# Splitting token rows before their norm is known, and moving half of each gather behind four weight blocks

## What is computed

```python
h = rms_norm(x, norm_ffn_g)                   # x * rsqrt(mean(x*x) + EPS) * g
logits = h @ w_router + b_router              # 32 experts
top_v, top_e = top_k(logits, 4); gates = softmax(top_v)
# for each expert e, the rows of h that chose it:
hh = xb @ w1[e] + b1[e]; glu, lin = split(hh)     # w1[e]: 1024 x 2048
act = min(glu, 7) * sigmoid(1.702 * glu) * (clip(lin, -7, 7) + 1)
y = act @ w2[e] + b2[e]                       # w2[e]: 1024 x 1024
x += sum over the 4 experts of gate * y
```

## Time and profile before

| | |
|---|---|
| time, median of 3 runs | 1242.89 us (1242.62 to 1244.21) |
| profiled execution, time | 1242.38 us |
| profiled execution, span | 1240.7 us |
| PE busy | 1160.5 us, 94% of the span |
| DVE, ACT, POOL busy | 387.7, 232.3, 62.9 us |
| transfers | 466.52 MB, mean 376 GB/s over the span |

### The profile page before, as it was taken

The page is one execution under the profiler, slowest core; times in us unless marked ns, Lnnn a source line. Parts: engine busy times, 40 slices in busy tenths (PEclk is TensorE's granted clock), DMA queues, the critical chain, the costliest instruction groups (busy, mean ns, idle before and its releaser), DMA issues.

```text
span 1240.7 us, 16218 instructions
## 1 busy us (share of the span) xinstructions
PE 1160.5 (94%) x6549; PEld 577.8 (47%) x6549; DVE 387.7 (31%) x729; ACT 232.3 (19%) x405; POOL 62.9 (5%) x102
## 2 busy tenths in 40 slices
PE   7999999997999999999998989898989898989996
PEld 5778899887434344343333333332323232323332
DVE  3555768377221222212121213131121212121214
ACT  3342244144101111010111011110101110111012
POOL 5302001123000000000000000000000000000000
PEclk9999999997999999999999999999999999999999
DMA  9833399996899999999999999999999999999994
GB/s 312 258 129 102 113 327 340 360 346 263 327 428 428 427 428 429 428 428 429 428 428 429 429 427 428 429 428 428 429 428 428 429 429 428 428 429 428 428 428 169
DMA packets 79748, 466.52 MB, mean 376 GB/s; under 512 B 4384, under 2 KB 51008, under 8 KB 54912
## 3 DMA queue, kind: packets, MB, share of 16 engines
q1 hardware_dynamic: 72816, 455.36, 89.7%
q0 software_dynamic: 1504, 6.13, 1.5%
q10 hardware_dynamic: 5392, 4.54, 1.2%
HBM read 460.32 MB, written 5.70 MB: 376 GB/s over the span
## 4 chain that ended last, share of the span: by engine, by line
PE 65%; DMA 30%; DVE 2%; ACT 1%; issue 1%; SPq 0%; ACTq 0%; DVEq 0%
DMA ring<-w 30%; PE bank L1739 21%; PE bank L1774 12%; PE bank L1356 9%; PE bank L1526 5%; PE bank L1714 5%; PE bank L1694 4%; PE bank L1514 2%; PE bank L1758 1%; ACT rest L801 1%; PE bank L1695 1%; PE bank L1586 1%; DMA ring<-w_in 1%; PE bank L1611 1%; PE bank L1557 1%; PE bank L1570 1%
## 5 line engine op out<-in xcount | busy, mean ns | idle before, releaser
L1739 PE MATMUL bank<-ring,rest 128*64 128x512 f32 x2048 | 457.8, 595 | 38.1 <-DMA ring<-w 31.7
L1739 PEld LDWEIGHTS bank<-ring,rest 128*64 128x64 f32 x2048 | 142.7, 136 | 333.0 <-issue 256.0
L1774 PE MATMUL bank<-ring,rest 128*64 128x512 f32 x1024 | 226.8, 595 | 17.0 <-ACT rest L801 17.0
L1281 DVE TENSOR_SCALAR rest<-bank 128x512 f32<-128x512 f32 x32 | 22.1, 692 | 486.9 <-PE bank L1739 486.9
L1774 PEld LDWEIGHTS bank<-ring,rest 128*64 128x64 f32 x1024 | 71.3, 137 | 151.2 <-issue 134.9
L1260 DVE TENSOR_TENSOR rest<-rest,bank 128x512 f32<-128x512 f32 (+1 forms) x102 | 66.9, 680 | 227.8 <-PE bank L1714 227.7
L1356 PE MATMUL bank<-rest,ring 128*128 128x288 f32 (+1 forms) x512 | 125.4, 405 | 8.5 <-DMA ring<-w_in 8.5
L797 ACT ACTIVATE rest<-rest 128x512 f32<-128x512 f32 x32 | 20.2, 630 | 523.4 <-DVE rest L1281 523.4
L1356 PEld LDWEIGHTS bank<-rest,ring 128*128 128x128 f32 x512 | 97.6, 192 | 33.9 <-DMA ring<-w_in 8.5
L1714 PE MATMUL bank<-rest 128*128 128x512 f32 (+1 forms) x204 | 98.4, 611 | 1.3 <-ACT rest L809 1.3
L809 ACT COPY rest<-bank 64x512 f32<-64x512 f32 x64 | 37.1, 580 | 225.2 <-PE bank L1774 224.5
(11 more groups left out here) (292 smaller groups left out, 712.8 us busy)
## 6 DMA issues: line engine op xcount, KB each, us to landing
ring<-w SPq DMA_DIRECT2D x192, 2048.0 KB, 33.5
ring<-w_in SPq DMA_DIRECT2D x12, 1024.0 KB, 12.0
ring<-k_t SPq DMA_DIRECT2D x8, 1024.0 KB, 12.3
ring<-v_c SPq DMA_DIRECT2D x8, 1024.0 KB, 7.2
ring<-w_xk SPq DMA_DIRECT2D x4, 1024.0 KB, 4.9
ring<-w_xv SPq DMA_DIRECT2D x4, 1024.0 KB, 4.9
ring<-w_out SPq DMA_DIRECT2D x4, 1024.0 KB, 7.6
ring<-w_xq SPq DMA_DIRECT2D x4, 1024.0 KB, 12.6
```

The source lines that it names most:

```text
L1739: last = t.matmul(out, slots[:, k, :], w[:, col], start=False, stop=(k == KT - 1))
L1774: last = t.matmul(ps[2][CAP * ds:CAP * ds + CAP, :], actT[:, at:at + CAP], w[:, b, 512 * ds:512 * ds + 512], start=(a == 0 and b == 0), st ...
```

## The change

The rows are split as they are, without the norm's factor. The factor of each token is itself split into three bf16 parts by POOL, spread over rows (`r_rows`), and brought to the slots by a further block of matmuls with the same `sel`: it lands in bank 5, ACT copies it to `r_slot`, and DVE multiplies by gain and factor while it evacuates the gather, both banks now. The first half of the columns is split while the output projection still runs; for this the copies of the bias's split go from DVE to ACT. The sums of squares are finished by DVE and PE needs one matmul for each group of tokens. The gather is two calls: `gather(0)`, with the factor's block in it, where the whole gather stood, and `gather(1)` behind the fourth unit of w1 of the pair's first expert, ahead of `combine`.

```diff
+        hx = [m(at, 3 * HALF).bitcast(BF16).rearrange("p (s t d) -> p s t d", s=3, t=2) for at in (8448, 0)]
+        hx_c = [m(at + 3 * HALF, HALF // 2).bitcast(BF16) for at in (8448, 0)]
+        hx_hi = [[hx[half][:, 0, 0, :], hx[half][:, 0, 1, :], hx_c[half]] for half in range(2)]
...
+        r_slot = m(3328, P)
+        r_part = m(3456, 5).bitcast(BF16)[:, 0:3 * TT].rearrange("p (s t) -> p s t", s=3)
+        r_rest = m(3464, TT)
+        r_rows = m(6752, 384).bitcast(BF16).rearrange("p (s t m) -> p s t m", s=3, t=2)
+        r_rows_c = m(7136, 64).bitcast(BF16)
...
+            pool.wait_ge(yrs_done, 1)
+            link(pool.tensor_copy(r_part[:, 0, :], yrs))
+            link(pool.tensor_tensor(r_rest, yrs, r_part[:, 0, :], ALU.subtract))
+            link(pool.tensor_copy(r_part[:, 1, :], r_rest))
+            link(pool.tensor_tensor(r_part[:, 2, :], r_rest, r_part[:, 1, :], ALU.subtract))
+            link(pool.tensor_copy(r_rows, r_part[:, :, 0:2].unsqueeze(3).to_broadcast([P, 3, 2, P])))
+            for part in range(COPIES):
+                q = slice(TS * part, TS * part + TS)
+                pool.tensor_copy(r_rows_c[q], r_part[q, part, 2:3].to_broadcast([TS, P])).then_inc(r_rows_done, 1)
+                pool.wait_ge(r_rows_done, part + 1)
...
+            a.copy(b1s[0:96], b1f[0:96]).then_inc(b1_split, 1)
+            def part_of_bias(sub, rows_b, done):
+                act_e.wait_ge(b1_sub, sub)
+                a.copy(b1s[rows_b], b1f[rows_b]).then_inc(done, 1)
+            def upper_rows(n):
+                half, tt = n // TT, n % TT
+                R = ROWS_C[tt]
+                if half == 0:
+                    act_e.wait_ge(y_ev, n + 1)
+                    src = y[0:R, tt, 0:HALF]
+                else:
+                    act_e.wait_ge(y_ps, n + 1)
+                    src = ps[Y_BANK[n]][0:R, :]
+                a.copy(hx_hi[half][tt][0:R, :], src).then_inc(h_hi, 1)
+            def middle_rows(n):
...
+                elif k == 4:
+                    act_e.wait_ge(b1_split, 4)
+                    upper_rows(0)
+                    upper_rows(1)
+                elif k == 5:
+                    middle_rows(0)
+                    middle_rows(1)
+                    upper_rows(2)
+                elif k == 6:
+                    middle_rows(2)
...
+            a.activation(yrs, ps[L_BANK[0]][:, NE:NE + TT], ACT.Sqrt, bias=eps, scale=1.0 / D).then_inc(std_done, 1)
+            for n in range(TT, 2 * TT):
+                upper_rows(n)
+            act_e.wait_ge(logits_in, 2)
+            a.activation(gate, gate, ACT.Exp).then_inc(logits_exp, 1)
+            def slot_scales(nth):
+                act_e.wait_ge(rs_ps, nth)
+                a.copy(r_slot, ps[5][:, 0:P]).then_inc(rs_done, 1)
...
-                act_e.wait_ge(xg_ps, 2 * nth - 1)
-                for k in range(KT // 2):
-                    last = a.activation(xg[parity][:, k, :], ps[4][:, k * P:(k + 1) * P], ACT.Copy, scale=gain_k[:, k:k + 1])
-                last.then_inc(xg_done_a, 1)
...
+                a.copy(y[0:R, tt, HALF:D], ps[Y_BANK[TT + tt]][0:R, :]).then_inc(y_ev, 1)
+                if tt == 0:
+                    slot_scales(1)
+            for n in range(TT, 2 * TT):
+                middle_rows(n)
...
+                elif c == 4:
                     x_rows(range(2))
-                if c == 6:
+                elif c == 5:
+                    rest_part(0)
+                    rest_part(1)
                     x_rows(range(2, TT))
-            dve.wait_ge(y_std, TT)
+                    third_part(0)
+                    third_part(1)
+                    dve.wait_ge(b1_split, 4)
+                    v.memset(selGT, 0.0).then_inc(selgt_zero, 1)
+                elif c == 6:
+                    rest_part(2)
+                    third_part(2)
+            dve.wait_ge(rsq_done, KT)
+            dve.wait_ge(rsq_sum, KT - 2)
+            copies = sq_c.rearrange("p (a t) -> p a t", t=TS)
+            first, last_sq = (sq_r[:, k, SEQ:T].unsqueeze(1).to_broadcast([P, P // TS, TS]) for k in (0, KT - 1))
+            v.tensor_tensor(copies, first, last_sq, ALU.add).then_inc(rsq_sum, 1)
+            v.tensor_tensor(sq_r[:, 0, 0:SEQ], sq_r[:, 0, 0:SEQ], sq_r[:, KT - 1, 0:SEQ], ALU.add).then_inc(rsq_sum, 1)
...
+            def evac_gather(nth, parity, half):
+                dve.wait_ge(xg_ps, 2 * nth - 1 + half)
+                if half == 0:
+                    dve.wait_ge(rs_done, nth)
+                for k in range(4 * half, 4 * half + 4):
+                    last = v.scalar_tensor_tensor(xg[parity][:, k, :], ps[4 + half][:, (k % 4) * P:(k % 4 + 1) * P],
+                                                  gain_k[:, k:k + 1], r_slot, ALU.mult, ALU.mult)
+                last.then_inc(xg_done_hi if half else xg_done_lo, 1)
...
+            for n in range(TT, 2 * TT):
+                rest_part(n)
+            dve.wait_ge(wr_in, 48)
+            evac_gather(1, 0, 0)
+            for n in range(TT, 2 * TT):
+                third_part(n)
+            link(v.tensor_scalar(place[:, :, NE:NE + 2], place[:, :, 0:2], -float(CAP), None, ALU.add))
...
-                        dve.wait_ge(xg_ps, g * BODY + j + 2)
+                        evac_gather(pair + 1, (j // 2) % 2, 1)
...
-                        evac_gather(g * (BODY // 2) + j // 2 + 2, (j // 2 + 1) % 2)
+                        evac_gather(pair + 2, (j // 2 + 1) % 2, 0)
...
+                q = sq_r[:, 0, tt * P:(tt + 1) * P] if tt < 2 else sq_c
+                last = t.matmul(ps[L_BANK[0]][:, NE + tt:NE + tt + 1], q, ones[:, 0:1], start=True, stop=True)
...
+                    if half == 0 and d == 1:
+                        slot_scales()
+                last.then_inc(xg_ps, 1)
+            def slot_scales():
+                for tt in range(2):
+                    for part in range(3):
+                        t.matmul(ps[5][:, 0:P], r_rows[:, part, tt, :], sel[:, tt, :], start=(tt == 0 and part == 0), stop=False)
+                t.matmul(ps[5][:, 0:P], r_rows_c[0:COPIES * TS, :], sel[0:COPIES * TS, 2, :], start=False,
+                         stop=True).then_inc(rs_ps, 1)
             pe.wait_ge(sel_done, 1)
-            for half in range(2):
-                pe.wait_ge(h_split, TT * (half + 1))
-                gather([half])
-            pe.wait_ge(y_ev, 2 * TT)
+            pe.wait_ge(h_split, TT)
+            pe.wait_ge(r_rows_done, COPIES)
+            gather(0)
             pe.wait_ge(gates_done, 1)
             for tt in range(TT):
                 last = t.transpose(ps[7][0:NE, tt * P:(tt + 1) * P], gates[:, tt, :], ident)
...
-                            pe.wait_ge(xg_done_v if k else xg_done_a, g * (BODY // 2) + j // 2 + 1)
+                            pe.wait_ge(xg_done_hi if k else xg_done_lo, g * (BODY // 2) + j // 2 + 1)
...
+                            if j % 2 == 0:
+                                pe.wait_ge(selgt_done, pair + r + 1)
+                                gather(1)
                             pe.wait_ge(outp_done, 2 * (n + 1))
                             if j % 2 == 0:
...
-                        gather()
+                        gather(0)
...
-                        pe.wait_ge(xg_done_a, g * (BODY // 2) + j // 2 + 2)
+                        pe.wait_ge(xg_done_lo, g * (BODY // 2) + j // 2 + 2)
```

More of the change, by code:

```diff
@@ L233, in hybrid_decoder_step @@
         b1f = m(8448, SLOT)
-        glu, lin, sig, act = (m(7680 + 512 * i, 512) for i in range(4))
-        actT = m(9728, 512)
+        glu, lin, sig = (m(1792 + 512 * i, 512) for i in range(3))
+        actT, act = m(7200, 512), m(7712, 512)
+        r_slot = m(3328, P)
[3 more added lines that the diff above has]
+        r_rows_c = m(7136, 64).bitcast(BF16)
         selGT = m(10240, 384)
@@ L629, in _ @@
             act_e.wait_ge(bn_done, 1)
-            a.activation(lrs, mv[:, :, 1], ACT.Sqrt, bias=eps).then_inc(bn_std, 1)
+            a.activation(lrs, mv[:, :, 1], ACT.Sqrt, bias=eps).then_inc(std_done, 1)
             token_rows(ktok, ktok_s, 2 * TT)
@@ L742, in _ @@
-            act_e.wait_ge(rsq_sum, KT - 2)
-            a.copy(copies(sq_c, 0), sq_r[:, 0, SEQ:T].unsqueeze(1).to_broadcast([P, COPIES, TS])).then_inc(rsq_done, 1)
+                elif k == 2:
+                    part_of_bias(2, slice(64, 96), b1_split)
+                elif k == 3:
+                    part_of_bias(3, slice(64, 96), b1_split)
+                elif k == 4:
[8 more added lines that the diff above has]
+                    middle_rows(2)
@@ L747, in _ @@
             for tt in range(TT):
                 R = ROWS_C[tt]
-                a.activation(yrs[0:R, tt:tt + 1], ps[L_BANK[tt]][0:R, NE:NE + 1], ACT.Sqrt, bias=eps[0:R],
-                             scale=1.0 / D).then_inc(y_std, 1)
-            act_e.wait_ge(yrs_done, 1)
-            act_e.wait_ge(y_ev, TT)
-            for tt in range(TT):
-                R = ROWS_C[tt]
```

(51 more changed lines are left out.)

167 lines of the change are left out of this document (74 added, 93 removed).

## The result

The changed kernel takes 1267.74 us (median of 4 runs, 1266.07 to 1268.24), against 1243.04 us (1242.62 to 1244.21) for the kernel before beside it: a ratio of 1.0194, 95% interval 1.0180 to 1.0209. It is slower by 24 to 25 us. The forecast was 1242.7 in a range up to 1248.

A forecast was written before the change was run, and what follows sets the result against it. The weight stream was taken as the bound to the end; -2.7 us at the start and +2.5 in the first pair made -0.2, 1242.2 against the profiled execution, 1242.7 as the runs' median; 8-in-10 range 1239.7 to 1248.

The forecast's parts named there:

- inside a pair: In each pair of experts: gather blocks inside w1 and later transposes add 2.5 us, giving 56.8, under the stream's 58.73.
- The threshold: In the loop: 3.2 us more per pair allowed before PE takes over from the weight stream.
- a wait of 0.9: Behind w1 in a pair's first expert: the transposes start 0.9 us later (0.8 to 1.1), behind DVE's queued evacuation.
- Rival 3: In the loop: evacuation behind `act` takes twice its rows, a pair costs 3.7 more, PE takes over: 1250; chance 0.11.
- The clock at the entry: Ahead of the first w1: PE's clock falling in some 3 us of idle time costs 0.9 us, bounds 0 and 2.3.
- rival 2: Ahead of the loop: POOL stretched to 301.5, w1 at low clock, +1.0 there and +2.5 a pair: 1246.4; chance 0.12.
- The start: At the loop's entry: first w1 at 307.3 instead of 310.91; in effect 308.2 with the clock, 2.7 us earlier.
- POOL's chain: Ahead of the gather: eight operations making the factor's parts, 1.9 us for seven small ones, 1.3 for the wide copy.
- the ports: In POOL's operations ahead of the gather: 1.0 us added for DVE working on SBUF beside them, end at 299.2.
- rival 1: At the entry: POOL hidden under `sel`, clock up, w1 at 305.4 (-5.5), a pair costs 2.3: 1239.7; chance 0.20.
- The load of b2: On POOL ahead of the loop, moved behind its chain: lands by 305 to 308.3, at most 1 us of harm.

The follow-up runs named there:

- The idle matmuls: The changed kernel plus 36 matmuls whose result nothing reads, behind `gather(0)` in each pair's first expert: 1248.21 us, ratio 1.0026 to the kernel before.

## Why the prediction was wrong

**The step that failed** is "inside a pair": "+2.5 us a pair, 56.8, still under 58.73. So fifteen pairs of it cost nothing". The +2.5 was right; the work and the wait came to +2.43. What was missing is what the wait does to the clock: behind 1.97 us of idle time the 32 matmuls of w2 ran partly at 1.2 GHz, +1.3 to +1.7 us in most pairs, +2.9 in three of them, and +1.83 on average. With both, a pair took 58.6 us, 4.26 more than before. The threshold that the prediction had worked out itself was 3.2 more, and beyond it each tenth counts sixteen times. The idle matmuls showed it by taking away nothing but the gap. I had priced the clock at one place, the entry, where I saw an idle time of 3 us, and not at the other, where I had just worked out a wait of 0.9 behind a gather cut from eight blocks to five.

**Rival 3** had the outcome, PE taking over, at 0.11, and by another mechanism: an evacuation of twice its duration. It took 1.13 us for four, below the 1.25 I had taken. Its threshold was right, its price (7.8 us) was a third of the real one. The chance was too small for a margin of 0.7 us a pair with the clock left out.

**The clock at the entry** was taken as +0.9 with 2.3 as the upper bound; it came to 9.30 - 6.87 = 2.43, at the bound. The shorter gather had brought the clock up as well, to 1.00 in 307 to 310. It fell in the 3.72 us of idle time behind it, before PE began again, and stayed at 0.50 to 316:

```profile
309.00:310.00 1.00, 0.00 (x0) 1.00 0.04 12
310.00:311.00 1.00, 0.00 (x0) 0.51 0.00 0
```

So the prediction had the case and its size, as rival 2, and gave it too little weight.

**The start** was forecast 3.6 us earlier and came 1.2 later. The miss of 4.8 is the delay of the residuals, 4.55 us (292.06 to 296.61), nearly to the tenth. The prediction began its sum at the sums of squares and never looked at what the moved copies and subtractions do to DVE ahead of it. From the last residual on the sum held, but as a total: 312.08 - 4.55 = 307.5 against 307.3. The thirds ended 0.5 us sooner than it had them (310.71 - 4.55 = 306.2 against 306.65), and the bias matmuls at the low clock took 0.5 longer (1.06 instead of 0.55). That these two cancel is luck.

**POOL's chain** was priced at 3.2 us and 1.0 for the ports. It took 3.0 us (from 299.72), with the wide copy at the lower bound:

```profile
300.78 0.82 POOL L571 COPY rest<-rest 128x768 bf16<-128x768 bf16 x1
301.67 1.08 POOL L574 COPY rest<-rest 32x128 bf16<-32x128 bf16 x3
```

It ended at 302.75, hidden beside `sel`, as rival 1 had it, and the 1.0 us was not there. The Trainium skill (SBUF — State Buffer, section "SBUF: two separate sides") has a DVE operation with two SBUF inputs and a GpSimd operation that reads SBUF lock each other out. Further ahead in the same trace POOL's rows agree: its copy of 96 columns took 2.38 us from 273.40 instead of 0.26, beside DVE's subtraction from 273.37 to 275.65. In the chain such operations met for 0.1 to 0.2 us at a time only (`chosen` from 301.47, the subtraction from 301.64, `sel` from 302.64); the DVE operations took 0.26, 0.25 and 0.56 us, as in the kernel before, and of POOL's copies one took 0.38 instead of 0.29. So the price of the ports was wrong for this place, and the run hardly tests the rule.

**The load of b2** was said to do at most 1 us of harm. In the changed kernel it did none, because the split rows came later still; once these were out of the way it was worth 2.9 us of idle time at the entry. A load moved behind a chain has its price at whatever comes to wait for it.

What stays open, besides the 0.4 us above: why the same idle time of 0.84 us was followed by a low clock in 3 to 5 pairs and not in the others, and why b1 landed up to 2.2 us apart.

## What to carry to other kernels

Where a change makes PE wait, price the wait and what the clock does to the work behind it, for every pass of the loop, and compare the sum with the margin to the stream; over the threshold each microsecond a pair costs sixteen here. A dead wait in the loop is shortened by giving the result another bank (1.97 to 0.84 us here), or made harmless by idle matmuls. Ahead of a long stretch of PE work these may also keep its first microseconds at full clock: behind 32 of them, and behind 24 with no gap, the first w1 was at full clock; behind 14 with a gap of 2.87 us it was not. When copies move between engines, follow each queue from the first operation moved, not from where the new chain begins.

## What the runs showed of the hardware

The granted clock fell behind much shorter idle times than I expected. In the loop, with five blocks of narrow bf16 matmuls ahead and 0.7 us more of idle time behind four transposes, 1.97 us of idle time lowered it in 16 of 16 pairs, 1.32 us (behind four blocks) in 10, 0.84 us in 3 to 5, 0.39 us (behind nine blocks) in none. These are the pairs in which w2 of the first expert took 8.4 us or more on PE's timeline; in all others it took 7.09. In the changed kernel the fall never came in the 1.97 us themselves, in the ten pairs looked at: it came in the transposes, in the idle time behind them, or up to 0.9 us into w2, when PE was busy again; so the loss stands in the rows of matmuls that have nothing wrong with them.

The Trainium skill (TensorE: Matmul & The Clock Gate, section "A second HAM failure mode: psum-queue depth-cycling") tells of a kernel in which PE stands for short moments between groups of matmuls, often enough that the clock goes up and down, and throughput is lost between the bursts. The runs agree in this, and the loss stands in w2's own rows here: a mean of 658 ns beside 595. The same page's section "HAM oscillation — how this bites in real kernels" explains the loss by single long gaps; by that alone w2 would have run at full clock here.
